# First attention: the last projections and the first output products on other ticks

## What is computed

```python
h = rms_norm(x, norm_mix_pre[l])
proj = h @ w_in[l]
qa, ka, va, qb, kb, vb = jnp.split(proj, SPLITS, axis=-1)
qa = apply_rope(rms_norm(qa...), ang_axial); ka = apply_rope(rms_norm(ka...), ang_axial)
out_a = global_attention(qa, ka, va)
qb = apply_rope(qb..., ang_1d); kb = apply_rope(kb..., ang_1d)
out_b = window_attention(qb, kb, vb, sink_b[l])
mixed = jnp.concatenate([rms_norm(out_a, group_norm_a[l]),
                         rms_norm(out_b, group_norm_b[l])], axis=-1) @ w_out[l]
x = x + rms_norm(mixed, norm_mix_post[l])
...
```

## Time and profile before

| what | value |
| --- | --- |
| median of 3 runs | 1095.09 us |
| profiled execution, first to last instruction (span) | 1094.1 us |
| busy PE, PEld, DVE | 1065.5, 939.3, 885.8 us |
| busy ACT, POOL | 666.9, 186.2 us |
| mean granted TensorE clock | 0.997 |
| chain that ended last: PE, DVE, ACT, issue | 84%, 7%, 5%, 2% |
| steps of the first attention (L1247) | 42.6 to 168.1 us |

### The profile page before, as it was taken

The page is one execution under the profiler, slowest core; times in us unless marked ns, Lnnn a source line. Parts: engine busy times, 40 slices in busy tenths (PEclk is TensorE's granted clock), DMA queues, the critical chain, the costliest instruction groups (busy, mean ns, idle before and its releaser), DMA issues.

```text
span 1094.1 us, 18024 instructions
## 1 busy us (share of the span) xinstructions
PE 1065.5 (97%) x6544; PEld 939.3 (86%) x6544; DVE 885.8 (81%) x1448; ACT 666.9 (61%) x1179; POOL 186.2 (17%) x239
## 2 busy tenths in 40 slices
PE   8999988999999999999999998999999999999997
PEld 6688876998999999888888777778899999998885
DVE  6888885798988888888684778666689889879876
ACT  7787785476555555656683477545445555566664
POOL 1486744011001111000000103300001111100000
PEclk9999999999999999999999999999999999999999
DMA  7423321766765676886536721045356676776553
GB/s 285 114 77 81 92 60 38 243 126 191 202 158 190 175 189 209 194 246 205 190 126 214 180 58 39 21 110 179 96 136 183 205 176 181 203 183 214 189 177 123
DMA packets 51320, 171.17 MB, mean 156 GB/s; under 512 B 6432, under 2 KB 7072, under 8 KB 51104
## 3 DMA queue, kind: packets, MB, share of 16 engines
q1 hardware_dynamic: 37296, 122.56, 34.3%
q0 software_dynamic: 13312, 46.14, 19.4%
q10 hardware_dynamic: 624, 1.31, 0.4%
HBM read 162.64 MB, written 48.23 MB: 193 GB/s over the span
## 4 chain that ended last, share of the span: by engine, by line
PE 84%; DVE 7%; ACT 5%; issue 2%; POOL 1%; DMA 1%; ACTq 0%; SPq 0%; DVEq 0%; POOLq 0%
PE bank L2090 11%; PE bank L2092 11%; PE bank L2091 11%; PE bank L2651 6%; PE bank L2653 6%; PE bank L2652 6%; PE bank L583 6%; PE bank L584 6%; PE bank L585 6%; PE bank L1148 2%; PE bank L1138 2%; PE bank L1093 1%; PE bank L1094 1%; PE bank L1095 1%; DVE wl L506 1%
## 5 line engine op out<-in xcount | busy, mean ns | idle before, releaser
L506 DVE TENSOR_TENSOR wl<-raw,wh 128x1024 fp32r<-128x1024 f32 (+1 forms) x144 | 169.6, 1184 | 63.1 <-ACT wh L493 61.5
L493 ACT ACTIVATE wh<-raw 128x1024 fp32r<-128x1024 f32 (+1 forms) x145 | 145.7, 1010 | 114.1 <-PE bank L2653 52.9
L2090 PE MATMUL bank<-h,wh 128*128 128x256 f32 x576 | 163.2, 283 | 2.2 <-DVE sw L2270 2.2
L2092 PE MATMUL bank<-h,wl 128*128 128x256 f32 x576 | 163.0, 283 | 0.0
L2091 PE MATMUL bank<-h,wh 128*128 128x256 f32 x576 | 163.0, 283 | 0.0
L2091 PE MATMUL bank<-hl,wh 128*128 128x256 f32 x432 | 122.3, 283 | 0.0
L2092 PE MATMUL bank<-hh,wl 128*128 128x256 f32 x432 | 122.2, 283 | 0.0
L2090 PE MATMUL bank<-hh,wh 128*128 128x256 f32 x432 | 122.2, 283 | 0.0
L2651 PE MATMUL bank<-wh,high_tokens 128*128 128x512 f32 x308 | 121.2, 394 | 0.7 <-DVE wl L506 0.7
L2653 PE MATMUL bank<-wh,low_tokens 128*128 128x512 f32 x308 | 120.0, 390 | 0.0
L2652 PE MATMUL bank<-wl,high_tokens 128*128 128x512 f32 x308 | 120.0, 390 | 0.0
(11 more groups left out here) (337 smaller groups left out, 2660.8 us busy)
## 6 DMA issues: line engine op xcount, KB each, us to landing
raw<-weights SPq DMA_DIRECT2D x163, 512.0 KB, 4.2
down_weight_sums<-weights POOLq DMA_DIRECT2D x60, 512.0 KB, 6.0
raw<-down_weight_sums SPq DMA_DIRECT2D x40, 512.0 KB, 4.0
down_weight_sums<-down_weight_sums POOLq DMA_DIRECT2D x20, 512.0 KB, 4.7
xres<-x_t SPq DMA_DIRECT2D x8, 512.0 KB, 6.7
down_weight_sums<-weights POOLq DMA_DIRECT2D x12, 256.0 KB, 4.1
sw<-ta SPq DMA_DIRECT2D x36, 64.0 KB, 2.0
raw<-down_weight_sums SPq DMA_DIRECT2D x8, 256.0 KB, 2.6
```

What stands on the lines that cost most here:

```text
L493: act.activation(wh[:, j, b, n], raw[:, j, b, n], ACT.Copy).then_inc(high_split, 1)
L506: v.tensor_tensor(wl[:, j, b, :], raw[:, j, b, :], wh[:, j, b, :].bitcast(F32), ALU.subtract)\
L2090: pe.matmul(o, wh_half[:, h, k, :], high[:, k, :], start=first and k == 0, stop=False, skip_group_check=True)
L2092: ins = pe.matmul(o, wl_half[:, h, k, :], high[:, k, :], start=False, stop=k == HK - 1, skip_group_check=True)
```

## The change

It is one of order, with one buffer split in two.

- `PIECES`: tile 10 ran over ticks 30 to 35, tile 11 over ticks 36 to 41, with two pieces in ticks 32, 34, 37 and 39. Now tile 10 runs one piece a tick from 29 to 36, and tile 11 one piece a tick from 37 to 44. `END` of tile 11 becomes 44, so `vec_project1` of it moves from tick 42 to 45, its cosine from 44 to 46, sine and sum from 46 to 48, and its parting from ticks 49 and 50 to 50 and 51. Tile 10's projection moves from tick 36 to 37.
- `MIX`: mixed tiles 0 and 1 are made at ticks 42 and 44 in place of 49 and 50 (low parts at 43 and 45), mixed tile 2 at 50 in place of 51 (low part at 51). Tiles 3 to 7 stay.
- `OUT_PIECES`: the first eight pieces ran one a tick from 52 to 59. Now they stand at ticks 45, 46, 48, 50, 52, 54, 56 and 58.
- The low parts of mixed tiles 0 and 1 would lie on the rotary angles, which are still in use at tick 43. They get 4 KB where `hsq` lay, and wait for the last normed tile alone; the low parts of tiles 2 and 3 keep their place and wait for all tiles.

```diff
-for _p in range(KT * (len(IN1) - 5)):
+for _p in range(KT * (len(IN1) - 7)):
     PIECES.setdefault(2 + _p * 40 // 56, []).append((5 + _p // KT, _p % KT))
+for _k in range(KT):
+    PIECES.setdefault(29 + _k, []).append((10, _k))
+    PIECES.setdefault(37 + _k, []).append((11, _k))
...
-HIGH.update({(6, None): 19, (7, None): 26, (9, None): 34, (10, None): 43, (11, None): 49})
+HIGH.update({(6, None): 19, (7, None): 26, (9, None): 34, (10, None): 43, (11, None): 50})
...
-MIX.update({0: 49, 1: 50, 2: 51})
-
-OUT_PIECES = {52: [(0, 0)], 53: [(1, 0)], 54: [(0, 1)], 55: [(1, 1)], 56: [(0, 2)], 57: [(1, 2)], 58: [(0, 3)], 59: [(1, 3)],
+MIX.update({0: 42, 1: 44, 2: 50})
+
+OUT_PIECES = {45: [(0, 0)], 46: [(1, 0)], 48: [(0, 1)], 50: [(1, 1)], 52: [(0, 2)], 54: [(1, 2)], 56: [(0, 3)], 58: [(1, 3)],
...
-        mix_l0 = place("mix_l0", [P, 4, S], F32R, at=arena + 32 * KB)
+        mix_l01 = place("mix_l01", [P, 2, S], F32R, at=arena + 84 * KB)
+        mix_l23 = place("mix_l23", [P, 2, S], F32R, at=arena + 32 * KB)
...
-            return mix_l0[:, k, :] if k < 4 else mix_1[:, k - 4, 1, :]
+            return mix_l01[:, k, :] if k < 2 else mix_l23[:, k - 2, :] if k < 4 else mix_1[:, k - 4, 1, :]
...
-            if i < 4:
+            if i < 2:
+                v.wait_ge(f1.done, DONE_ORDER.index(NORMED[-1]) + 1)
+            elif i < 4:
                 v.wait_ge(f1.done, len(DONE_ORDER))
```

## The result

| | before | after |
|---|---|---|
| time, median | 1095.09 us (1094.62 to 1095.78, 6 runs) | 1099.36 us (1098.30 to 1103.59, 6 runs) |
| profiled execution, time | not on record | 1100.62 us |
| profiled execution, span | 1094.1 us | 1098.8 us |
| start of TensorE's turn in tick 64 | 168.36 us | 173.03 us |

The changed kernel is slower: ratio 1.0037, 95% interval [1.0025, 1.0048], where the forecast was 1092.6 us.

What follows compares the result with a forecast made beforehand. The bound was taken to go TensorE, VectorE and ScalarE together, then TensorE. The terms -1.5 - 0.3 + 0.6 + 0.5 - 0.9 + 0.9 - 2.4 + 0.6 gave -2.5 us, so 1092.6 us, range 1089.8 to 1096.0.

Steps and rivals of the forecast that it cites:

- (f): Tick 52: TensorE waits 2 us for the output piece one tick behind its mixed low part; +0.9 us, ends 0 and +2.
- the sentence on SyncE's queue: Tile 11's DMAs go three ticks and one tick later, with only one weight load between them; no cost was given.
- (a): Ticks 34 to 41: TensorE has less work and VectorE follows by its waits; -1.5 us, ends 0 and -2.07.
- (b): Ticks 42 and 43: VectorE's pauses shrink as ScalarE starts earlier but also makes mixed high 0; -0.3 us, ends 0 and -0.5.
- (c): Tile 11's projection leaves tick 42, which gains nothing, and costs VectorE at tick 45; +0.6 us, ends 0 and +0.6.
- (d): Ticks 43 to 45: added mixed parts make ScalarE late for tick 45's `pth`; +0.5 us, ends 0 and +1.2.
- (h): Four meetings of VectorE and GpSimd instructions, each costing up to 1 us or none; +0.6 us, ends 0 and +2.
- (e): Tick 50: ScalarE's parting of tile 11 stands behind `pth`, so VectorE's pause goes; -0.9 us, ends 0 and -0.94.
- (g): Ticks 55 to 63: with every second output piece gone, VectorE's waits lose their cause; -2.4 us, ends -2.5 and -1.2.
- The low clock behind tick 52: Rival: the wait at tick 52 brings a clock fall losing 1.7 us of work; -0.8 us, 1094.3 us; chance 0.16.
- The slower rival: TensorE stays at the lower clock in thin ticks 53 to 64; 10 us of it gives 1097.6 us; chance 0.07.
- The sum: All steps together: -2.5 us, a span of 1091.6 us with about 1 us around it, so 1092.6 us.

Runs made afterwards that it cites:

- the mended kernel: Changed kernel with SyncE issuing placings, swaps, then loads, and the output pieces of mixed tiles 2 and 3 at ticks 54, 55, 57, 59: 1095.31 us.
- the projection alone: Kernel before with only the projection part of the change (tiles 10 and 11): 1098.19 us, or 1096.6 us with SyncE's order mended.
- the kernel with the later pieces: Changed kernel with only the output pieces of mixed tiles 2 and 3 moved, to ticks 54, 55, 57, 59: 1096.02 us.
- the late placing: Changed kernel with SyncE's swaps ahead of loads, which put tile 10's placing DMAs behind tile 11's swap: 1102.22 us, or 1101.75 us with output pieces from tick 54.
- The kernel before with the late swap: Kernel before with only tile 10's swap DMAs issued at tick 37, behind that tick's weight load, in place of tick 36: 1096.47 us.
- the mended order: Changed kernel with only SyncE's order put right (placings, swaps, loads), output pieces as in the change: 1097.58 us.
- the mixed-and-output kernel: Kernel before with only the mixed tiles and output pieces of the change, projections as before: 1097.96 us.

## Why the prediction was wrong

The direction was wrong: -2.5 us were forecast, +4.3 measured, outside the range. The step that failed most is (f), the price of the piece at tick 52; the second is the sentence on SyncE's queue. By its steps:

- **(a) Ticks 34 to 41, -1.5.** Got -0.9. In the mended kernel TensorE is 1.9 us earlier at tick 40, VectorE 0.5. Of the waits in the earlier trace rows the 0.59 at tick 35 fell to 0.32, and the next one, for `pth` in the same tick, rose from 0.13 to 0.82 (first row below); the 0.38 and 0.58 of tick 40 became 0.26, and the split at tick 37 grew from 1.20 to 1.40 us beside GpSimd's scaling. Even the 0.9 is not steady: four other profiles with the same order to tick 42 have -0.2 to -0.5, with a split of 1.6 to 1.9 us at tick 40 for 1.2, and all of them stand at +0.4 by tick 44, as the mended kernel does.
- **(b), (c) Ticks 42 and 43.** These had the sign wrong. I had mixed high 0 as a small thing of 0.6 us on ScalarE. It stands ahead of `pth` of tick 43, and with the projection of tile 11 gone from VectorE's tick 42, VectorE waits 1.27 us for that `pth` where the earlier trace rows had 0.29 (1.26 in after; 0.90 with the mixed tiles alone, 0.65 with the projection alone). VectorE's two waits and ScalarE's two instructions in the mended kernel:

```profile
118.28 0.42 DVE L1261 TENSOR_TENSOR ptl<-bank,pth 128x256 fp32r<-128x256 f32 x1 [0.82 <-ACT pth L1392]
...
133.94 0.69 DVE L1261 TENSOR_TENSOR ptl<-bank,pth 128x512 fp32r<-128x512 f32 x1 [1.27 <-ACT pth L1392]
```

```profile
132.58 0.71 ACT L1573 ACTIVATE mix_h<-xres,cols 128x512 fp32r<-128x512 f32 x1
133.31 0.60 ACT L1392 ACTIVATE pth<-bank 128x512 fp32r<-128x512 f32 x1
```

- **(d), (h) Ticks 43 to 46.** The mended kernel is 3.6 us longer from tick 42 to tick 47 where my steps made +2.4; VectorE's pauses there are 1.9 us for 0.6, most of it the 1.27 above. The meetings at tick 45 are 0.3 us each on two mixed parts, near what (h) allowed and far from its upper end.
- **The turn of tick 44.** This is the step that I had settled with a sentence: I looked at tile 11's DMAs in SyncE's queue, and not at tile 10's, whose last piece moved by one tick as well. I had read the earlier trace rows as a wait for GpSimd and the DMA behind it as in time. What it cost: VectorE enters tick 47 1.1 us later in after than in the mended kernel, and the time falls by 0.7 to 1.8 us where the swap alone is put right (three pairs of kernels). Part of the 1.1 us is the slow landing in that execution, by the rows of the kernel with the later pieces above.
- **(e) Tick 50, -0.9.** ScalarE no longer stands for `tb`, but the gain did not come: the parting and the mixed high part now stand ahead of a `pth` one tick later, and VectorE waits there 1.03 us. From tick 47 to tick 52 VectorE gained 0.8 us, about what the mixed low part that left these ticks is worth.
- **(f) Tick 52, +0.9.** The mechanism was right, its price was not. The wait was forecast at 2 us between 0.8 and 3.6, and is 3.01, 3.33, 2.83 and 2.88 us in the four kernels with the piece: of the 3.6 the added pieces took off 0.3 to 0.8 us, not the 1.5 that I had put down. And I priced it for VectorE at 0.9 us, as if VectorE's own work would cover the rest. In after ticks 52 to 55 took 5.8 us on VectorE for 4.3 before, though one mixed low part (0.66 us) had left them, which is 2.2 us for this step. Its worth in the time is 2.3, 2.7 and 3.3 us in three pairs of kernels that differ in the places of these four pieces alone; in the pair with the late placing it is 0.5, with overlapping intervals. The step's own end was +2.
- **(g) Ticks 55 to 63, -2.4.** Got -1.5, and -1.6 in the mended kernel, and less than half of that is the pieces. The profile of before had its fall just ahead of these ticks, and TensorE was full until 160 us. The kernel before with the late swap has the same output pieces and no fall: these ticks take 11.8 us in it, 12.8 in before and 11.1 in the mended kernel, with 1.7, 2.6 and 1.2 us of pauses on VectorE. So by one profile of each the pieces were worth about 0.7 us. I had taken pauses behind a fall for pauses behind pieces; what is left is `pth` behind a turn, with or without a piece.
- **The low clock behind tick 52** was the first rival, at 0.16, and a fall stands around or behind the wait in each of the four profiles with the held piece. Before had one at that place as well, so in after it is not a fall more; but falls are more frequent with the piece: of the executions, a mean clock of 0.999 or above was had by 1 of 12 and 1 of 11 with it, and by 6 of 11 and 8 of 11 of the same kernels with the later pieces (30 of 87 in before). It should have hung on my step (f). The slower rival, 5 us and more of low clock in the thin ticks 53 to 64, did not come: the one fall ends at 160.3 us.
- **The sum.** The time outside the span is not about 1 us but 1.8 (1100.62 and 1098.8 in after; 1.7 to 1.9 in every execution of the experiments). The forecast time is the median less 2.5 and isn't touched by it; the span that belongs to 1092.6 us would have been 1090.8, not 1091.6.

The largest failing is (f) with what it brings; the second is the queue order at tick 37 that no step had. With both mended, the forecast would still have been too good by 2.1 us at tick 63 and by 2.7 in the time, by (a), (b), (e) and (g).

What was shown: the four output pieces in their first places cost 2.3 to 3.3 us, the late swap costs 0.7 to 1.8 us (four pairs; 1.0 where it is added to before), and without both the change is worth 0.0 us, give or take 1. Not shown with the same weight: how the cost of the held piece divides between the wait and the clock. Executions of the same mean clock can be set side by side. Three of after had 0.997 and took 1098.3 to 1098.7 us, where 44 of before with 0.997 took 1094.5 to 1096.9, 1095.8 in the mean: 2.7 of the 4.3 us stand at the same clock. With the held piece one execution of the mended order had 0.999 and took 1096.25 us, where the mended kernel takes 1094.9 to 1095.5 at 0.998 and above; one of the mixed-and-output kernel had 0.999 and took 1096.6, where it takes 1094.7 to 1095.4 with the later pieces. That makes about 1 to 1.5 us for the wait, and the rest of the 2.3 to 2.7 for the falls: an estimate from two executions.

## What to carry to other kernels

When a table moves the last piece of a tile by even one tick, list every instruction that is timed from it, DMAs first, and look at what each one passes in its queue; a 64 KB DMA behind a load that waits for its buffer is as late as the load. A matmul that is issued one tick behind the VectorE instruction that feeds it holds all the scores behind it in TensorE's queue: here one tick behind waited 2.8 to 3.3 us, two ticks behind waited nothing at tick 45 and 0.58 us at tick 52 of before, and three ticks behind waited nothing at tick 54. A wait of VectorE for another engine is only worth what the next wait behind it leaves: before it is put down as gain, read the slack of the following two hand-offs. And pauses behind a fall of the clock belong to the fall; read them in a profile that has none.

## What the runs showed of the hardware

- Five profiled executions have a TensorE wait of 2.8 us or more (after and four experiments), and in all of them the granted clock was at its lower level around or behind it, for 3.4 to 6.8 us: from 151.2 us in the mixed-and-output kernel, whose wait ended at 152.35, and from 156.9 us in after, whose wait ended at 155.87. A long wait is not needed for a fall: of the nine without one, three have a fall at that place (before at 149.1 us, where the longest wait ahead of it was 1.02 us, and the two kernels with the projection part alone, behind 1.56 us), and six have none, one of them with a wait of 2.06 us. The same 1.65 us of wait at tick 53 stand in five executions, four of which show no fall there. The Trainium skill, page "TensorE: Matmul & The Clock Gate", section "A second HAM failure mode: psum-queue depth-cycling", describes a kernel whose clock goes to and fro because of very short pauses between groups of matmuls; here no profile shows more than two falls in the attention, of 3.4 or 6.8 us each.
- A fall can stand in code that two kernels share (40.8 to 44.2 us in after, about the same place in the pieces-only kernel, and not in before). Of the 1.74 us by which everything behind it is later, 0.11 stood ahead of it, so it cost 1.6. Over 87 executions of before, those with a mean clock of 0.999 took 1095.0 us in the mean and those with 0.997 took 1095.8. One profiled execution of each kernel is not enough to compare spans to 2 us.
- Four DMAs of 64 KB landed 3.0 us after issue (median) behind a 512 KB load in after and 2.0 us ahead of it in before. Single ones vary: the last of the four took 3.29 us in after, 1.99 in the kernel with the later pieces though it was behind the load too, and 3.60 in the mended kernel though it was ahead of it.
- VectorE's mixed part (two SBUF inputs) beside GpSimd's scaling: 1.03 to 1.07 us for 0.75, and the scaling of four blocks 2.91 for 2.06. In the kernel with tile 4's part moved to ticks 49 and 50, beside the scaling of 148.29 to 150.78 us, it took 0.78 us at 149.09 us, and the block scaled at 149.30 us took 1.02 for 0.59: there GpSimd alone paid.
